# Two norms moved within the projection steps of a two-block transformer kernel

## The reference

```python
# first block
x = x + 0.5 * swiglu(rms_norm(x, g_ffn1), ...)
q, k, v, u, mq = split(rms_norm(x, g_mix) @ w_in)
y_attn = sliding_window_attention(rope(rms(q)), rope(rms(k)), v, sinks)
y_conv = conformer_conv(u)                      # gate, 31 taps, layer norm, silu
mk, mv = split(rms_norm(mem, g_mem) @ w_mem_kv) # mem: 256 x 1024
y_mem  = memory_cross_attention(rms(mq), rms(mk), mv)
x = x + concat(y_attn, y_conv, y_mem) @ w_out
x = x + 0.5 * swiglu(rms_norm(x, g_ffn2), ...)
# second block, layer 0 (layer 1 has a short convolution as its mixer)
q, k, v, qi, ki, wi = split(h @ w_in)           # h: modulated norm of x
ki = rope(layer_norm(ki)); qi = rope(qi)
score = sum_h wi[h] * relu(qi[h] @ ki)          # causal
sel = top_k(score, 128)                         # each query attends to these keys
y = attention(rope(rms(q)), rope(rms(k)), v, sel) @ w_out
x = x + g1 * y;  x = x + g2 * swiglu(...)
```

## Time and profile before

| | |
|---|---|
| median of three runs | 2204.99 us (2201.59 to 2208.15) |
| the profiled execution | 2208.4 us, span 2206.7 us |
| granted clock of PE, mean of the span | 0.986 |
| PE busy | 98% |
| DVE, ACT, POOL busy | 55%, 35%, 11% |
| first mixer, norm to last tile | about 399 to 499 us |
| second mixer, norm to last tile | about 983 to 1117 us |

### The profile page before, as it was taken

The page is one execution under the profiler, slowest core; times in us unless marked ns, Lnnn a source line. Parts: engine busy times, 40 slices in busy tenths (PEclk is TensorE's granted clock), DMA queues, the critical chain, the costliest instruction groups (busy, mean ns, idle before and its releaser), DMA issues.

```text
span 2206.7 us, 28945 instructions
## 1 busy us (share of the span) xinstructions
PE 2160.9 (98%) x10222; PEld 1763.4 (80%) x10226; DVE 1212.3 (55%) x1760; ACT 783.4 (35%) x1081; POOL 234.3 (11%) x237
## 2 busy tenths in 40 slices
PE   7999999899999999999989999999999999999999
PEld 6888888687888888877767888888888878888887
DVE  6655444695565554455787475553456457333332
ACT  5222233446542223333445342222333224222221
POOL 0000200560200020013210200000000000000000
PEclk8999999999999999999989999999999999999999
DMA  4665233320245542333210135552332222222232
GB/s 160 197 188 182 90 92 100 110 93 20 86 134 182 188 155 79 91 104 101 87 48 1 67 117 187 181 171 76 91 109 96 102 89 87 95 95 95 78 95 83
DMA packets 75733, 242.96 MB, mean 110 GB/s; under 512 B 9328, under 2 KB 9584, under 8 KB 75536
## 3 DMA queue, kind: packets, MB, share of 16 engines
q1 hardware_dynamic: 61376, 189.61, 26.5%
q0 software_dynamic: 14288, 52.44, 7.7%
HBM read 235.65 MB, written 2.10 MB: 108 GB/s over the span
## 4 chain that ended last, share of the span: by engine, by line
PE 90%; DVE 7%; ACT 1%; issue 1%; DMA 0%; ACTq 0%; SPq 0%; DVEq 0%
PE ps L659 27%; PE ps L661 27%; PE ps L660 27%; PE ps L967 2%; PE ps L925 1%; PE ps L946 1%; PE ps L745 1%; DVE tmp L1564 1%; DVE score L1982 1%; DVE h_lo L1593 1%; DVE top L1980 1%; PE ps L928 1%; DVE tmp L1585 0%; PE ps L1092 0%; DVE w_lo L1521 0%
## 5 line engine op out<-in xcount | busy, mean ns | idle before, releaser
L659 PE MATMUL ps<-h_hi,w_hi 128*128 128x512 f32 x1888 | 746.8, 396 | 17.1 <-issue 8.1
L661 PE MATMUL ps<-h_hi,w_lo 128*128 128x512 f32 x1888 | 738.7, 391 | 0.0
L660 PE MATMUL ps<-h_lo,w_hi 128*128 128x512 f32 x1888 | 738.2, 391 | 0.0
L1521 DVE TENSOR_TENSOR w_lo<-w_raw,w_hi 128x1024 fp32r<-128x1024 f32 x336 | 413.2, 1231 | 439.6 <-ACT w_hi L1173 429.0
L1173 ACT ACTIVATE w_hi<-w_raw 128x1024 fp32r<-128x1024 f32 x383 | 402.6, 1052 | 257.4 <-PE ps L661 256.0
L659 PEld LDWEIGHTS ps<-h_hi,w_hi 128*128 128x128 f32 x1888 | 356.0, 189 | 99.6 <-issue 19.7
L661 PEld LDWEIGHTS ps<-h_hi,w_lo 128*128 128x128 f32 x1888 | 355.5, 188 | 76.5
L660 PEld LDWEIGHTS ps<-h_lo,w_hi 128*128 128x128 f32 x1888 | 356.2, 189 | 73.1
L659 PE MATMUL ps<-hid_hi,w_hi 128*128 128x512 f32 x704 | 278.4, 396 | 0.0
L660 PE MATMUL ps<-hid_lo,w_hi 128*128 128x512 f32 x704 | 278.4, 396 | 0.0
L661 PE MATMUL ps<-hid_hi,w_lo 128*128 128x512 f32 x704 | 278.4, 396 | 0.0
(11 more groups left out here) (303 smaller groups left out, 1749.3 us busy)
## 6 DMA issues: line engine op xcount, KB each, us to landing
ada_raw<-in_ada_w POOLq DMA_DIRECT2D x96, 512.0 KB, 4.2
w_raw<-in_gate SPq DMA_DIRECT2D x88, 512.0 KB, 3.5
w_raw<-in_up SPq DMA_DIRECT2D x88, 512.0 KB, 3.5
w_raw<-in_down SPq DMA_DIRECT2D x64, 384.0 KB, 3.0
w_raw<-in_down SPq DMA_DIRECT2D x64, 320.0 KB, 2.8
w_raw<-in_w_mix_c SPq DMA_DIRECT2D x24, 512.0 KB, 3.5
w_raw<-in_w_mix_b SPq DMA_DIRECT2D x17, 512.0 KB, 3.5
w_raw<-in_w_mix SPq DMA_DIRECT2D x16, 512.0 KB, 3.5
```

The costliest lines, as they stand in the source:

```text
L659: pe.matmul(dest, s_hi, m_hi, start=first and n == 0, stop=False)
L660: pe.matmul(dest, s_hi, m_lo, start=False, stop=False)
L661: mm = pe.matmul(dest, s_lo, m_hi, start=False, stop=last and n == len(pairs) - 1)
L1521: dve.tensor_tensor(chunk(w_lo, slot, WT), chunk(w_raw, slot, WT), f32(chunk(w_hi, slot, WT)), ALU.subtract).then_inc(w_lo_done, 1)
```

## The change

First mixer: POOL loads `mem` as before but squares and halves it inside its loop of splits, the square and the first halving behind the split of J+4 (and behind a wait for the whole norm, `h_lo_done`), the other two behind the split of J+5. The steps that follow move two steps on: PE's sum from tile 3 to 5 and spread from tile 5 to 7, ACT's root from step 4 to 6 and high part from 7 to 9, DVE's reciprocal from 5 to 7 and multiplication from 6 to 8, POOL's low part from J+10 to J+11. Two taps go from step 8 to step 6.

Second mixer: PE's sum of `ki` goes from tile 2, sixth group, to tile 3, third group; the turn of `wi` from tile 2 to tile 3, sixth group; the sum of squares from tile 3 to 4; the spread from tile 4 to 5. ACT keeps `wi` in step 3, and takes the root in step 4; DVE takes the reciprocal of ki at the end of step 4's rope instead of before it.

```diff
-        TAPS_AT = {2: 5, 3: 6, 4: 6, 5: 6, 6: 4, 7: 6, 8: 4, 9: 4, ...}
+        TAPS_AT = {2: 5, 3: 6, 4: 6, 5: 6, 6: 6, 7: 6, 8: 2, 9: 4, ...}
 # POOL, first mixer
-            pool.wait_ge(stage_in, 32)
-            pool.tensor_tensor(qA[:, :], memx[:, :], memx[:, :], ALU.mult).then_inc(g_misc.at("mem_sq"), 1)
-            for part, done, before in ((4, "mem_sum4", "mem_sq"), (2, "mem_sum2", "mem_sum4"), (1, "mem_sum", "mem_sum2")):
+            def halve_memory(part, done, before):
                 after(pool, g_misc, before)
                 pool.tensor_tensor(qA[:, 0:part * M], qA[:, 0:part * M], qA[:, part * M:2 * part * M], ALU.add)\
                     .then_inc(g_misc.at(done), 1)
             for j in range(LEAD, len(TILES_A) + KC):
                 split(first_job["mixA"] + j)
-                if j == 10:
+                if j == 4:
+                    pool.wait_ge(stage_in, 32)
+                    pool.wait_ge(h_lo_done, 2 * KC)
+                    pool.tensor_tensor(qA[:, :], memx[:, :], memx[:, :], ALU.mult).then_inc(g_misc.at("mem_sq"), 1)
+                    halve_memory(4, "mem_sum4", "mem_sq")
+                if j == 5:
+                    halve_memory(2, "mem_sum2", "mem_sum4")
+                    halve_memory(1, "mem_sum", "mem_sum2")
+                if j == 11:
                     after(pool, a_misc, "mem_hi")
 # PE, betweenA
-                if part == 1 and m == 3:
+                if part == 1 and m == 5:
                     after(pe, g_misc, "mem_sum")
-                if part == 1 and m == 5:
+                if part == 1 and m == 7:
                     after(pe, d_misc, "mem_rstd")
 # PE, betweenB
-                if part == 0 and m == 4:
+                if part == 0 and m == 5:
                     head_spread("ki")
-                if part == 1 and m == 2:
+                if part == 0 and m == 3:
                     after(pe, evac, "ki")
-                if part == 0 and is_token_major(TILES_B[m - 1]) and m > 2 or part == 1 and m == 2:
+                if part == 1 and m == 3:
+                    turn_tile(TILES_B, 1)
+                if part == 0 and is_token_major(TILES_B[m - 1]) and m > 2:
                     turn_tile(TILES_B, m - 1)
-                if part == 0 and m == 3:
+                if part == 0 and m == 4:
                     head_sum("ki", matsB)
 # ACT: mem_std m == 4 -> 6, mem_hi m == 7 -> 9; second mixer:
-                if t == "wi":
-                    keep_tile(t, m - 1, wi[:, :], WI_SCALE)
+                if m == 3:
+                    keep_tile("wi", 1, wi[:, :], WI_SCALE)
-                if m == 3:
+                if m == 4:
                     head_std("ki")
 # DVE: mem_rstd m == 5 -> 7, the memory's multiplication m == 6 -> 8; second mixer:
-                if n in h_rstd.value and m > 3:
+                if n in h_rstd.value and m > 4:
                     head_rstd(n)
...
+                if m == 4:
+                    head_rstd("ki")
```

More of the change, by code:

```diff
@@ L421, in build @@
         TOP_EARLY = sum(TOPS_AT.values())
-        TAPS_AT = {2: 5, 3: 6, 4: 6, 5: 6, 6: 4, 7: 6, 8: 4, 9: 4, 10: 4, 11: 4, 12: 4, 13: 4, 14: 3, 15: 2}
+        TAPS_AT = {2: 5, 3: 6, 4: 6, 5: 6, 6: 6, 7: 6, 8: 2, 9: 4, 10: 4, 11: 4, 12: 4, 13: 4, 14: 3, 15: 2}
         def index_slot(m, part):
@@ L1409, in _ @@
                     keep_tile(t, m - 1, values_place(mv, int(t[2]) * 2 * MT, 2 * MT))
-                if m == 4:
+                if m == 6:
                     after(act, p_misc, "mem_total")
@@ L1413, in _ @@
                         .then_inc(a_misc.at("mem_std"), 1)
-                if m == 7:
+                if m == 9:
                     after(act, d_misc, ("mem", KC - 1))
@@ L1908, in _ @@
                     head_rope(r, ropA, kA[:, :] if r == "kA" else chunk(qA, int(r[2])))
-                if m == 5:
+                if m == 7:
                     after(dve, a_misc, "mem_std")
                     dve.reciprocal(hrA[:, 64 + 40:64 + 40 + MT], hrA[:, 40:40 + MT]).then_inc(d_misc.at("mem_rstd"), 1)
-                if m == 6:
+                if m == 8:
                     after(dve, p_misc, "mem_spread")
```

## The result

The changed kernel takes 2201.36 us (median of 18 runs, 2196.05 to 2209.29); the kernel before, in as many runs beside it, 2209.97 (2201.59 to 2214.55). The ratio is 0.9972, 95% interval 0.9960 to 0.9984: 6.2 us faster (3.5 to 8.8). The forecast was a gain of 6.8 us and 2198.2 us. The gain of 6.8 is inside the interval. The time is 3.2 us over the forecast: 6.8 was subtracted from 2204.99, the median of three runs, which lies 5.0 us under that of the eighteen, and the two medians lie 8.6 apart, 1.8 more than 6.8.

A forecast was written before the change was run, and what follows sets the result against it. TensorE, busy 98% of the span, was taken as the bound, so only its waits and lower clock could give time. First mixer 2.6 (5.96 − 3.4) plus second 4.2 gives 6.8 us off 2204.99: 2198.2 us, range 2193 to 2203.5.

The forecast's parts named there:

- how the numbers follow: Last step, from forecast and rivals to chances: faster 0.47, no change 0.48, slower 0.05, with 0.3% (6.6 us) as the bound.
- sum of 6.8: Whole kernel: 2.6 us from the first mixer plus 4.2 from the second, giving 2198.2 us; chance 0.42.
- rival (a): First mixer: the wait for the swap is hidden and only PE's 0.45 us lost; gain 9.7, 2195.3 us; chance 0.25.
- Front of the first mixer: Norm takes 11.03 us instead of 16.99 once POOL's memory work moves behind it; gain 5.96 us.
- What is given back there: First mixer: DVE late at mk0's reciprocal, PE waits about 3 us and ends the mixer 3.4 us late, leaving 2.6.
- DVE's lateness: First mixer, at mk0's reciprocal: DVE 5.5 us late (3 to 7), from 3.5 + 1.5 + 0.5.
- wait for kA's swap: First mixer, kA's second rope multiply: DVE waits about 3.5 us (2.5 to 5), the swap issued at about 446.2.
- blocks beside POOL: First mixer: DVE's rope instructions held up beside POOL's work, 1.5 us plus 0.5 beside the split of J+9.
- rival (d): First mixer: SP's queue never back in step, DVE waits at all five ropes, 22.5 us in all; 2215 us; chance 0.06.
- rival (b): First mixer: PE's new pauses before kA's sum and mk0 lower the clock; total gain about 4.7, 2200.3 us; chance 0.22.
- Second mixer: PE's stops for `kraw` and `wi` and the lower clock go; gain 4.2 us (3.5 to 4.7).
- the key's rope: Second mixer, index key: done at 1026.0 to 1027, PE wants it at 1026.5; costs 0 to 0.6 us, 0.1 taken.

The follow-up runs named there:

- pool_old: Changed kernel with GpSimd's square of the memory and its halvings back ahead of the split of the fourth tile: 2205.02 us, ratio 0.9975 to the kernel before.
- kswap: Changed kernel with kA's half-swap one load earlier in SyncE's queue, behind the load of J+10: 2203.00 us, ratio 0.9960 to the kernel before.
- best3: `best2` with the three moved taps later, in step 15, behind the reciprocal of mk1: 2197.11 us, ratio 0.9949 to the kernel before.
- best1: `mhlate` plus the index key's reciprocal ahead of qi0's rope and its spread half a tile earlier: 2192.65 us, ratio 0.9927; run again 2193.69 us.
- a_only: Changed kernel with only the first mixer's part, the second mixer as before: 2209.59 us, ratio 0.9993 to the kernel before.
- best2: `best1` with kA's head sum and spread half a tile later and three taps moved from step 13 to 14: 2197.10 us, ratio 0.9955.
- mh12: Changed kernel with GpSimd's mh_lo one split later, behind the split of J+12: 2200.52 us in a single run.
- mhlate: Changed kernel with both kA's swap one load earlier and mh_lo one split later: 2193.46 us, ratio 0.9926 to the kernel before.
- b_only: Kernel before with only the second mixer's part of the change: 2202.93 us, ratio 0.9972 to the kernel before.

## Why the prediction was right and wrong

**What failed first is the last step, how the numbers follow.** I gave "no change" 0.48 and "faster" 0.47, though the sum of 6.8 and rival (a) lay beyond the bound, because I took less than 0.3% as something a measurement here can hardly tell. I had read the spread of three single runs (6.6 us) as the limit; a ratio over many runs is known better than one run. Eighteen runs a side tell it to 0.12%, and the interval (0.9960 to 0.9984) leaves "no change" out. The time was off by the base: the 18 runs of the kernel before lie 13 us apart, and the median of three of them was 5 us off. I allowed for 2 or 3. The profiled run (2208.4) was nearer to the truth than the median I subtracted from.

**Front of the first mixer: right.** Norm 11.02 us (11.0 said), 5.97 gained (5.96), PE's wait for kA's square 2.56 (2.5). `pool_old` shows that the POOL work's place does it.

**What is given back there: nearly the right sum, partly by luck.** `mk0`'s reciprocal stood at 495.8 (495.4 said), PE's wait was 2.60 (about 3 said), and the mixer gave 2.12 instead of 2.6. The terms behind DVE's lateness (5.5 said, 5.97 measured) were off in opposite directions. The wait for kA's swap was priced at 3.5 and put DVE back by 3.05: it waited 2.62, since the swap left at 445.7 instead of 446.2 in the terms of before, and came 0.4 late. The blocks beside POOL were priced at 2.0 and were 3.0: the fifteen rope instructions took 17.9 us together, 14.9 before.

One thing that `mh_lo` does was put at nothing. I priced it only as blocks for DVE's ropes. It also holds up the split of J+12, and with it a load and the swap of qA3 behind the load: rival (d)'s mechanism, in one place instead of five. I had it at 470 and it came there (464.33 + 6.02), since POOL idled 4.65 us in front of it for ACT's copy, which now stands two steps later; before, it idled for nothing there. But I didn't follow SP's queue on from it. In the changed kernel this costs nothing, because DVE is late by kA's swap anyway; `pool_old` and `kswap` show it as waits of 3.92 and 3.93 us. So the wait for kA's swap, which I held for the cause, was only the first of two.

**Clock behind the new pauses, rival (b): half right.** The stop at kA's sum did lower it (0.51 for 3 us). PE was ready for `mk0`'s reciprocal at 493.5 in the terms of before (490.04 − 2.60 + 6.02), not at 492.65, most likely by it. I had held it for hidden, and rightly as long as DVE was late. With DVE on time it counts: `best3`, with 0.53 and 0.82 us left of the stop and no low clock, has a mixer 2.2 us shorter than `best1`. The pause at `mk0` lowered it in `a_only` (2.60 us), and that at `mk1` in `best2` (2.05); the pause at `mk0` didn't in either execution of the changed kernel (2.60) nor in `kswap` (2.16), `mh12` (2.38) or `pool_old` (1.71). My sum for this rival took 0.6 off for a pause that it priced at 1.5, without a reason; in `a_only` the low clock cost 1.5 (93.76 against 92.25).

**Second mixer: 3.79 instead of 4.2.** Both waits and the low clock went. The term mis-sized is the key's rope: 0.1 said, 1.16 measured. My own bound had it done at 1026.0 to 1027; it was done at 1027.0, since both its last operations met a split of POOL, and PE was there at 1025.9 instead of 1026.5 (both in the terms of before). I took the early end of the bound without asking where POOL would be, though the row of before already showed 1.66 for one of them.

**Not in the prediction:** attention 2 and the way to the last norm, −0.89 and 2.16 in the one pair of profiles. The second is the execution, not the change: 544.07 became 541.91 here and is 544.12 in `mhlate`, whose code there is the same. Of the first this isn't shown (see `b_only`).

What stays open: why `best3` with the shorter mixer has no shorter time, and why `best1` gained 1.8 us more over the changed kernel than its mixers. The clock has a part in the first. The median clock of the twelve runs of `best3` is 0.987 (0.981 to 0.992), that of the twelve of `best1` 0.9895 (0.988 to 0.991), and the slowest runs of `best3` are those with the lowest clock (2207.99 us at 0.981). Whether where PE stops sets this, or chance does, one or two profiles of a kernel don't tell. The best version run is `best1`: 2192.65 and 2193.69 us, 0.7% under the kernel before; `mhlate`, at 2193.46, can't be told from it by the total.

## What to carry to other kernels

When a step moves inside an in-order queue, follow everything behind it through each queue that waits for it (here POOL's split, SP's load, the swap behind the load, DVE's rope, PE's spread), and after the first late one go on: a second may stand under its cover, and each cure alone then shows next to nothing (0.2 and 0.4 us here, 2.66 together). Put a short producer ahead of an instruction that will idle for a DMA anyway. Where executions differ by more than the change is worth, cut the span at fixed instructions and compare the stretch that the change touches; don't subtract a gain from the median of three runs, and don't take the spread of single runs for what many runs can tell.

## What the runs showed of the hardware

The differences between executions of one kernel go with stretches at TensorE's lower clock, some of them in places that change from run to run. The stretch behind the first mixer takes 486.5, 488.1 or 489.6 us. From 500 to 530 the windows show, for the kernel before, `mhlate` and `best1` in turn:

```profile
500.00:530.00 30.00, 29.78 (x209) 0.89 0.06 18
```

```profile
500.00:530.00 30.00, 29.83 (x235) 0.94 0.01 1
```

```profile
500.00:530.00 30.00, 29.84 (x249) 1.00 0.00 1
```

A longer, a shorter or no stretch at 1.2 GHz, at a cost of 3.1, 1.6 or nothing on top of the 486.5. The start of the kernel does the same (the clock of 10 to 20 us is 0.66 where the first norm comes at 405.56 and 1.00 where it comes at 401.75). Over the 18 runs of the changed kernel the mean clock orders the times: those at 0.990 took 2196.1 to 2197.6 us, those at 0.984 2208.0 to 2209.3.

An idle PE didn't always lower its clock: 2.60 us before `mk0` did in one of three executions. The stop of 2.56 us at kA's sum did in all eight that have it. A stop with matmuls put into it (0.53 us left of 2.56) left it at 1.00.
